# The convolution branch's projection in three passes, a fourth buffer for high weight parts, and VectorE work moved between stages, in a two-block layer stack

## The reference, cut to what matters

```python
mod = silu(c) @ w_ada + b_ada
h = rmsnorm(x, norm_g) * (1 + scale) + shift
rq, rk, rv, rg, xbc, dt_raw, z, fq, fk, fv, fg, f_raw = split(h @ w_in)
xbc = silu(causal_dwconv(xbc, conv_w, conv_b))          # 4 taps
mixed = concat([retention * silu(rg), rmsnorm(ssd * silu(z)), fox * silu(fg)])
x = x + gate * (mixed @ w_out)
```

```python
# GLU -> depthwise conv (31 taps) -> channel layernorm -> swish -> projection
conv = silu(layernorm(dwconv(a * sigmoid(g)))) @ w_conv_out       # 512 -> 1024
mlstm = (rmsnorm(h_fwd + h_bwd) * sigmoid(o_pre)) @ w_mlstm_out   # 4 heads of 256
attn = attention(q, k, v) @ w_attn_out                            # 8 heads, 2 for k and v
x = x + g1 * ((g_conv * conv + g_mlstm * mlstm + g_attn * attn) @ w_out)
x = x + g2 * conv_ffn(h)                                          # 1024 -> 2 x 2816 -> 1024
```

## Time and profile before

| | before |
|---|---|
| median of 3 runs | 2354.2 us (2354.12 to 2355.55) |
| the profiled execution | 2356.64 us, span 2354.8 us |
| granted TensorE clock, mean | 0.987 |
| PE busy | 2293.4 us (97%), 14962 matmuls |
| PEld, DVE, ACT, POOL busy | 81%, 60%, 41%, 5% |

### The profile page before, as it was taken

The page is one execution under the profiler, slowest core; times in us unless marked ns, Lnnn a source line. Parts: engine busy times, 40 slices in busy tenths (PEclk is TensorE's granted clock), DMA queues, the critical chain, the costliest instruction groups (busy, mean ns, idle before and its releaser), DMA issues.

```text
span 2354.8 us, 35094 instructions
## 1 busy us (share of the span) xinstructions
PE 2293.4 (97%) x14962; PEld 1908.9 (81%) x14962; DVE 1411.5 (60%) x2590; ACT 973.0 (41%) x1571; POOL 119.2 (5%) x95
## 2 busy tenths in 40 slices
PE   6999999999999999999999999999999999999999
PEld 4898888988877887776787677775877988998999
DVE  1467844667748676545344555555267757566984
ACT  2438633376524354352221332331244535544542
POOL 0000000000000032120000000000000133100000
PEclk8999999999999999999999999999999999999999
DMA  9794357863444111113332454332333311564553
GB/s 312 248 294 148 104 182 249 288 215 118 134 141 129 49 60 38 48 41 107 107 100 95 144 180 161 125 99 71 99 109 77 97 61 55 165 209 146 190 177 117
DMA packets 335532, 323.25 MB, mean 137 GB/s; under 512 B 28560, under 2 KB 334992, under 8 KB 335248
## 3 DMA queue, kind: packets, MB, share of 16 engines
q1 hardware_dynamic: 335376, 321.00, 43.2%
HBM read 319.93 MB, written 1.05 MB: 136 GB/s over the span
## 4 chain that ended last, share of the span: by engine, by line
PE 89%; DVE 6%; DMA 2%; ACT 2%; issue 0%; POOL 0%; SPq 0%; ACTq 0%
PE ps L746 88%; DVE parts L2031 1%; DMA ring<-w_ada 1%; ACT w_high L1508 1%; DMA ring<-w_in 1%; DVE arena L2416 1%; DVE arena L2572 1%; PE ps L1259 1%; POOL parts L1956 0%; DVE arena L2174 0%; DVE arena L2168 0%; SPq L677 0%; ACT arena L1618 0%; DVE parts L2071 0%; DVE arena L2542 0%
## 5 line engine op out<-in xcount | busy, mean ns | idle before, releaser
L746 PE MATMUL ps<-parts,w_high 128*128 128x256 f32 (+1 forms) x6384 | 1135.3, 327 | 5.2 <-DVE arena L2612 2.3
L746 PEld LDWEIGHTS ps<-parts,w_high 128*128 128x128 f32 x6384 | 950.3, 189 | 137.0 <-issue 27.7
L746 PE MATMUL ps<-parts,parts 128*128 128x256 f32 (+1 forms) x3384 | 609.6, 321 | 6.9 <-DVE parts L2387 2.6
L1508 ACT ACTIVATE w_high<-ring 128x1024 fp32r<-128x1024 f32 (+2 forms) x426 | 433.0, 1026 | 411.0 <-PE ps L746 327.5
L746 PEld LDWEIGHTS ps<-parts,parts 128*128 128x128 f32 x3384 | 502.6, 189 | 63.1 <-DVE parts L2031 3.1
L2387 DVE TENSOR_TENSOR parts<-ring,w_high 128x1024 fp32r<-128x1024 f32 (+2 forms) x262 | 304.6, 1169 | 231.4 <-ACT w_high L1508 230.9
L1956 POOL TENSOR_TENSOR parts<-ring,w_high 128x512 fp32r<-128x512 f32 x88 | 118.3, 1372 | 1899.5 <-ACT w_high L1508 1899.5
L746 PE MATMUL ps<-arena 128*64 128x256 f32 (+7 forms) x928 | 184.0, 397 | 6.5 <-DVE arena L2612 5.9
L746 PEld LDWEIGHTS ps<-arena 128*128 128x128 f32 (+2 forms) x928 | 123.5, 171 | 53.1 <-issue 19.8
L2031 DVE TENSOR_TENSOR parts<-ring,w_high 128x1024 fp32r<-128x1024 f32 x88 | 104.8, 1221 | 96.6 <-ACT w_high L1508 96.6
L2416 DVE SCALAR_TENSOR_TENSOR arena<-arena,cols 128x512 f32<-128x512 f32 (+1 forms) x240 | 158.2, 659 | 6.0
(11 more groups left out here) (270 smaller groups left out, 1794.6 us busy)
## 6 DMA issues: line engine op xcount, KB each, us to landing
ring<-w_in SPq DMA_DIRECT2D x118, 1024.0 KB, 5.3
ring<-ada_w SPq DMA_DIRECT2D x48, 1024.0 KB, 5.5
ring<-ffn_w_up SPq DMA_DIRECT2D x44, 1024.0 KB, 5.1
ring<-w_ada SPq DMA_DIRECT2D x24, 1024.0 KB, 7.5
ring<-w_out SPq DMA_DIRECT2D x16, 1024.0 KB, 5.1
ring<-ffn_w_down SPq DMA_DIRECT2D x16, 1024.0 KB, 5.2
ring<-w_out SPq DMA_DIRECT2D x16, 512.0 KB, 4.4
ring<-w_mlstm_out SPq DMA_DIRECT2D x8, 1024.0 KB, 5.2
```

The source lines that it names most:

```text
L746: return tensor.matmul(o, a, b, start=first, stop=last)
L1508: scalar.activation(half_high(m), half_raw(m), ACT.Copy).then_inc(*a.step(("w_high", m)))
```

## The change

It has these parts.

- Constants: `ones` is one column (it is broadcast in the operand), `blk` two columns, `dup0` and `dup1` are gone, and `ada_y` is one buffer rather than two, with a wait of ACT for the batch before. The first load of constants falls from 294 to 167 columns and the second from 1408 to 1026.
- `SPLIT_BUFS` goes from 3 to 4. With the constants this moves `arena` from byte 120,288 to byte 121,344 of each partition, a multiple of 64. Nothing ahead of `w_high` moves, and `cst` stays a multiple of 64.
- The convolution branch's projection (`bo`, b = 0) goes by three passes: DVE makes `ln_high` and `ln_low` ahead of the gate copies and eight low weight halves of four tiles for each layer, ACT eight more high halves. The mLSTM branch's parts are made at n = 8 and 10 rather than 4 and 6.
- Gates: ACT rounds weights `SPLIT_BUFS - 1` halves ahead.
- First stack: ACT's silu of the convolution's tiles 0 to 7 goes between the `fk` evictions; DVE makes the first low half of `rq` ahead of the low activation tiles.
- Taps: none in the mLSTM stage; in layer 0 eight more early ones among the mix stage's last, in layer 1 five rather than four after each attention job.
- Layer 1: the low part of the second half of each head's `mo` strip moves from POOL to DVE, at the head's start.

```diff
@@ -72,7 +72,7 @@
 _at = 0
-for _name, _n in [("ident", P), ("ones", P), ("freq", 1), ("eps", 1), ("eps_eps", 1), ("eps64", 1), ("pick", 32), ("sign", 1), ("cneg", 1), ("blk", P), ("rota", P), ("rotb", P), ("dup0", P), ("dup1", P),
+for _name, _n in [("ident", P), ("ones", 1), ("freq", 1), ("eps", 1), ("eps_eps", 1), ("eps64", 1), ("pick", 32), ("sign", 1), ("cneg", 1), ("blk", 2), ("rota", P), ("rotb", P), 
                   ("low", P), ("up", P), ("axc", SEQ), ("axs", SEQ)]:
...
@@ -312,7 +310,7 @@
-SPLIT_BUFS = 3
+SPLIT_BUFS = 4
 GATES_WHOLE = 3
@@ -333,7 +331,7 @@
         return "gate", name[1]
-    if name[0] == "bo" and name[2]:
+    if name[0] == "bo":
         return "gate", name[1]
@@ -424,7 +422,7 @@
         csel = sb("csel", [P, KT, ADA_SHIFT + 32])
-        ada_y = sb("ada_y", [P, 2, 256])
+        ada_y = sb("ada_y", [P, 256])
         mod1 = sb("mod1", [P, DEPTH, 24])
@@ -457,6 +455,7 @@
         a_parts = under([P, 2, TT])[0:ROWS, :, :]
+        ln_high, ln_low = mh_high[0], merged_high[0]
         laid.append(1)
...
@@ -633,7 +632,7 @@
                 return KT // 2, 2 * P
-            if name[0] == "bo" and name[2] == 1:
+            if name[0] == "bo" and name[2] < 2:
                 return 4, P
...
@@ -1372,30 +1371,25 @@
                     pe.wait_ge(*when(("lnsq", l, t)))
-                    i = mm(u[:, lo:TT], ones, mv_sq[:, t, lo:TT], t == 0, t == DW_T - 1)
+                    i = mm(u[:, lo:TT], ones.to_broadcast([P, P]), mv_sq[:, t, lo:TT], t == 0, t == DW_T - 1)
                 i.then_inc(*pe.step(("full", ("lnq", l))))
+                ln_tiles = [ln_high[:, k, :] for k in range(4)]
                 att_tiles = [att_high[:, k, :] for k in range(4)]
                 mh_tiles = [mh_high[k // 4][:, k % 4, :] for k in range(KT)]
-                for b, (high, low, parts) in enumerate(((None, None, None), (att_tiles, att_low, ("att", l)), (mh_tiles, mh_low, ("mh", l)))):
+                for b, (high, low, parts) in enumerate(((ln_tiles, ln_low, ("ln", l)), (att_tiles, att_low, ("att", l)), (mh_tiles, mh_low, ("mh", l)))):
                     for s in range(4):
...
                         name = ("bo", l, b, s)
-                        wt = take(name)
+                        take(name)
                         for j in range(2):
                             u = unit(("bo", l, b, 2 * s + j))
-                            if b:
-                                i = split_strip(u[:, lo:TT], name, j, lo, low, high=high, parts=parts)
-                                i.then_inc(*pe.step(("used_half", half_no[name, j]), ("full", ("bo", l, b, 2 * s + j)), ("used", name)))
-                                continue
-                            for k in range(4):
-                                pe.wait_ge(*when(("ln", l, k)))
-                                i = mm(u[:, lo:TT], wt[:, k, j * P:(j + 1) * P], cacc[:, k, lo:TT], k == 0, k == 3)
-                            i.then_inc(*pe.step(("full", ("bo", l, b, 2 * s + j)), ("used", name)))
+                            i = split_strip(u[:, lo:TT], name, j, lo, low, high=high, parts=parts)
+                            i.then_inc(*pe.step(("used_half", half_no[name, j]), ("full", ("bo", l, b, 2 * s + j)), ("used", name)))
                 for s in range(4):
@@ -1468,7 +1462,9 @@
                 a.wait_ge(*when(full(("ada_y", batch))))
-                scalar.activation(ada_y[:, batch % 2, :], bank(("ada_y", batch))[:, 0:256], ACT.Copy).then_inc(*a.step(("ada_y", batch), read(("ada_y", batch))))
+                if batch:
+                    a.wait_ge(*when(full(("ada_m", batch - 1))))
+                scalar.activation(ada_y[:, :], bank(("ada_y", batch))[:, 0:256], ACT.Copy).then_inc(*a.step(("ada_y", batch), read(("ada_y", batch))))
@@ -1588,14 +1584,20 @@
+                def convolved(t0, t1):
+
+                    for t in range(t0, t1):
+                        a.wait_ge(*when(("conv", l, t)))
+                        scalar.activation(xconv[:, t, :], xconv[:, t, :], ACT.Silu, bias=col(g1, "conv_b")[:, t:t + 1]).then_inc(*a.step(("xconv", l, t)))
+
+                convolved(0, 4)
                 for s in range(2):
...
                     scalar.activation(fkT[:, 2 * s:2 * s + 2, :], bank(("fk", l, s)).rearrange("p (a b) -> p a b", a=2), ACT.Copy).then_inc(*a.step(("fk", l, s), read(("fk", l, s))))
-                for t in range(CONV_T):
-                    a.wait_ge(*when(("conv", l, t)))
-                    scalar.activation(xconv[:, t, :], xconv[:, t, :], ACT.Silu, bias=col(g1, "conv_b")[:, t:t + 1]).then_inc(*a.step(("xconv", l, t)))
+                    convolved(4 + 2 * s, 6 + 2 * s)
+                convolved(8, CONV_T)
                 for b in range(2):
@@ -1888,7 +1890,7 @@
                     gate = (0, 2, 1)[b]
-                    high_parts(("gate", l), half_no[("bg", l, b, n // 2 % 4), n % 2] + 2)
+                    high_parts(("gate", l), half_no[("bg", l, b, n // 2 % 4), n % 2] + SPLIT_BUFS - 1)
                     a.wait_ge(*when(full(("bg", l, b, t))))
@@ -1900,6 +1902,7 @@
                     scalar.activation(cacc[:, t, lo:TT], cacc[:, t, lo:TT], ACT.Silu, scale=col(g2, "conv_ln_w_2")[:, t:t + 1], bias=col(g2, "conv_ln_b_2")[:, t:t + 1]).then_inc(*a.step(("ln", l, t)))
+                high_parts(("gate", l), half_no[("bo", l, 0, 1), 0])
                 for t in range(4, 3 * KT):
@@ -1950,6 +1953,8 @@
                 for n in range(first, last_half["back", l] + 1):
+                    if l and split_halves[n][0][0] == "mo" and split_halves[n][1]:
+                        continue
                     p.wait_ge(*when(("w_high", n)))
@@ -2065,12 +2070,14 @@
+                weights_low("rq", 0, (0,))
                 v.wait_ge(*when(full(("fv", l, 1))))
...
-                for part, s in (("rq", 0), ("rq", 1), ("rk", 0), ("rk", 1), ("xbc", 0), ("xbc", 1)):
+                weights_low("rq", 0, (1,))
+                for part, s in (("rq", 1), ("rk", 0), ("rk", 1), ("xbc", 0), ("xbc", 1)):
                     weights_low(part, s)
@@ -2499,6 +2506,7 @@
                     low_part(mix_half + n)
+                    early_taps(0 if lo else 4)
                 axc, axs = const("axc"), const("axs")
@@ -2551,7 +2559,7 @@
                     att_prob(n)
-                    taps(4 if lo else 2)
+                    taps(5 if lo else 2)
                     if n > 2 and n % 2:
@@ -2615,6 +2623,8 @@
                         m_exponents(0, 1)
+                    if l:
+                        low_part(half_no[("mo", l, hd), 1])
                     m_weights(hd, 0)
@@ -2622,7 +2632,6 @@
                         m_exponents(hd + 1, 0)
-                    taps(DW_T * DW_K - taps_done[0] if hd == M_HEADS - 1 else 3)
                     m_outs(hd, 1)
@@ -2661,6 +2670,13 @@
+                for t in range(DW_T):
+                    v.wait_ge(*when(("ln", l, t)))
+                    vector.tensor_copy(ln_high[:, t, lo:TT], cacc[:, t, lo:TT]).then_inc(*v.step(("h_high", "ln", l, t)))
+                    v.wait_ge(*when(("h_high", "ln", l, t)))
+                    vector.tensor_tensor(ln_low[:, t, lo:TT], cacc[:, t, lo:TT], ln_high[:, t, lo:TT].bitcast(F32), ALU.subtract).then_inc(*v.step(("h_low", "ln", l, t)))
+                for j in range(2):
+                    low_part(half_no[("bo", l, 0, 0), j])
                 for t in range(KT):
@@ -2673,8 +2689,8 @@
                             branch_parts("att", aq, 0, att_high, att_low)
-                        if n in (4, 6):
-                            branch_parts("mh", mq, 4 * (n // 6), mh_high[n // 6], mh_low)
+                        if n in (8, 10):
+                            branch_parts("mh", mq, 4 * (n // 10), mh_high[n // 10], mh_low)
                         v.wait_ge(*when(full(("bo", l, b, t))))
@@ -2695,7 +2711,7 @@
                             vector.tensor_tensor(merged_low[:, t, lo:TT], o, high.bitcast(F32), ALU.subtract).then_inc(*v.step(("h_low", "wo2", l, t)))
-                        if 3 <= n // 2 < 11:
+                        if n // 2 < 11:
                             low_part(half_no[("bo", l, (n // 2 + 1) // 4, (n // 2 + 1) % 4), n % 2])
```

More of the change, by code:

```diff
@@ L94, in shape_constants @@
     put("ones", 1.0)
-    put("blk", (p[:, None] // 64 == p[None, :] // 64))
+    put("blk", (p[:, None] // 64 == np.arange(2)[None, :]))
     for name, half in (("rota", 64), ("rotb", 32)):
@@ L492, in program @@
         eps = const("eps")
-        one_col = ones[:, 0:1]
+        one_col = ones
         pick = const("pick")
@@ L801, in ada_sum @@
                 for t in range(2):
-                    i = mm(u[:, 24 * t:24 * t + 24], ada_y[:, batch % 2, t * P:(t + 1) * P], pick[:, 0:24])
+                    i = mm(u[:, 24 * t:24 * t + 24], ada_y[:, t * P:(t + 1) * P], pick[:, 0:24])
                 i.then_inc(*pe.step(("full", ("ada_m", batch))))
@@ L820, in group_sum @@
                 for g in range(4):
```

(5 more changed lines are left out.)

3 lines of the change are left out of this document (removed).

## The result

The changed kernel takes 2339.9 us (median of 4, 2338.7 to 2342.1) against 2354.4: a ratio of 0.9937, with a 95% interval of 0.9926 to 0.9949, so 12 to 17 us less. The prediction was 2324 with a range of 2317 to 2343; its rival (a) said 2340. The profiled execution spans 2338.6 us, 16.2 less than before.

What follows compares the result with a forecast made beforehand. The prediction took TensorE, busy 97% of the span, as the bound. Steps 1 to 6 sum to -14.2 us and step 7 adds -16: -30.2 from the profiled 2356.6 gives 2326.4, a median of 2324, range 2317 to 2343.

Steps and rivals of the forecast that it cites:

- rival (a): The start of `arena` doesn't matter, so the gain of step 7 is missing: 2340 us; chance 0.28.
- step 7: `arena` put on a multiple of 64 bytes: 512-column fp32r matmuls reading it fall to 0.227 us; -16 us, bounds -20 and 0.
- step 6: First stack, silus between the `fk` evictions: VectorE's convolution ends its last tile as late as before; -0.5 us, bounds -2 and 0.
- Steps 1 and 2: Convolution branch's projection of b = 0, fp32 replaced by fp32r passes: -5.4 us in layer 0, -0.5 in layer 1.
- Step 3: Taps out of layer 0's mLSTM stage: TensorE's waits for the outputs shrink; -5.5 us, bounds -6.0 and -4.
- Step 4: Layer 1's mLSTM stage: waits of 2.3 us go, low parts on VectorE cost +2.4; taken as 0, bounds -2 and +2.5.
- Step 5: First low weights of `rq`: their subtraction moves into VectorE's idle time, 1.15 us gained per layer; -2.3 us, bounds 0 and -2.5.
- Rival (c): A TensorE that waits less gets less clock; 2% less mean clock gives 2370 us; chance 0.04.

## Why the prediction was right and wrong

The sign was right; the size was twice too large: -30.2 us forecast, -14.8 measured. The step that failed is step 7 (-16 forecast, -5.9 measured for the shift alone), and step 6 added to it (-0.5 forecast, +5 in the traces). These two make up the miss. The time lay inside the range only because the range had been stretched to reach rival (a). Its ends do not follow from the terms: with every term at its best the sum is 2314 and not 2317, and without the shift and every term at its worst it is 2349 and not 2343.

**Step 7, the operands' place: wrong rule, so wrong size.** The prediction put `arena` on a multiple of 64 bytes and gave every stage the fast pace, -16 us. The shift alone gave -5.9. The trace of before held two facts and I joined them wrongly: that 0.2267 and 0.2327 follow the operand was right, and holds in all twelve kernels; that 32 against 33 pieces of 64 bytes explains it was a number that happened to fit, and only roughly: with two thirds of the operands off it would make 2.1%, and the rows say 2.6%. The runs put another rule in its place: 512-column fp32r matmuls take 0.227 us when the activation tile and the weights start at the same place modulo 256 bytes, 0.229 to 0.234 when they don't. By that rule the change brought only up's tiles into agreement (128 and 128) and left gates and down at 0 against 128, mix at 192 against 128. The part about 256 columns stands: there agreement costs, 0.120 against 0.118 to 0.119. The true size of the idea was near what was claimed, -13.3 to -14.4 us in the kernel before with the tiles really in agreement, so the phenomenon was sized well and its condition was not. The counter-rule that was weighed, lines of 16 bytes in the Trainium skill's page "SBUF — State Buffer", section "Specifications (TRN2)", is no better: read as the prediction read it, no shift of 32 or 128 bytes should matter, and each did. Why agreement matters (for instance whether loads of weights and reads of tiles meet) no run here shows.

**Steps 1 and 2, three passes for b = 0: right.** -5.4 and -0.5 forecast. The two traces before and after drift apart by 5.3 us over layer 0's three groups and by 0.5 over layer 1's. In layer 1 VectorE was late as foreseen, 0.68 us at the first low weights against 0.9. The cover in layer 0 held, and it is as thin as was said. VectorE's first two low weight halves and TensorE's first matmul with low weights, after:

```profile
1063.57 1.29 DVE L2394 TENSOR_TENSOR parts<-ring,w_high 128x512 fp32r<-128x512 f32 x2
...
1064.44 1.10 PE L745 MATMUL ps<-parts 128*128 128x512 f32 x4
```

The first half ends at about 1064.2, 0.2 us before it is read; a tenth was forecast. The undo run gives +2.4 us by its time, with an interval that holds both nothing and the 5.9.

**Step 3, taps in layer 0: right.** -5.5 forecast; the traces move apart by 2.2, 2.2 and 1.4, 5.8 in all, and together again by as much in the undo. Another 1.5 us between the second and the third place are not counted: there the trace of before has a granted clock of 0.72 (978 to 984 us), and the kernel with the shift alone, which runs the same instructions, has 1.00, so it is this execution's chance.

**Step 4, layer 1's mLSTM: near in the sum, but both parts too small.** The taps' waits were 2.3 us by the row, and taking them back costs 3.7 in the trace. The low part on VectorE was put at +2.4 and measures +3.8 at its places in the trace, +5.6 by the ratio: 1.1 of the subtraction's 4.9 us were covered, where half had been put down as covered. Forecast 0, with -2 to +2.5 as bounds; the traces before and after show +0.9 over this stage. That the sum came out is luck, since two misses of 1.4 us cancelled.

**Step 5: right.** -2.3 forecast; the traces step by -1.2 at each of the two places.

**Step 6: wrong sign.** -0.5 forecast; putting the silus back gains 7.5 us by the ratio and 5.0 in the traces. The prediction saw that VectorE's convolution ends no sooner and concluded that nothing is lost. It missed that TensorE's wait, though no later at its end, becomes one long idle stretch instead of many short ones, after which the granted clock is at its lower level for some microseconds. The two traces end 9.0 us apart. They place 2.4 and 2.6 at the silus of the two layers; 2.6 more lie in the first 50 us, where the three kernels above that undo another part and keep the new order are 1.8 to 2.1 us ahead of the changed kernel's trace as well, and the rest in stretches with a clock below 1.00. So what is over 5.0 is not the silus' as far as the traces show.

**Rival (c)** did not come: the mean clock was 0.985 after and 0.987 before. Where it did fall, at the silus, it fell behind a longer single wait. **Rival (a)** named the right time, 2340, and that was luck. The place does matter, and its gain of about 6 us was cancelled by step 6's loss.

**What the parts make together.** Undone one at a time, the effects by the ratios are: shift -5.9 (in the kernel before), b = 0 -2.4, taps -10.6, mo lows +5.6, silus +7.5, and step 5's -2.3 from the trace: -8.1, where the whole is -14.8. Four of these are differences known to some 5 us each, and an error in the changed kernel's ratio enters the sum four times, so the gap of 7 is within the noise. The places in the traces fit better: shift -5.9 (by the ratio), b = 0 -5.8, taps of layer 0 -5.8, layer 1's mLSTM stage +0.9, step 5 -2.3, silus +5.0, together -13.9. The constants' smaller loads and the batch's single `ada_y` were not tried alone.

## What to carry to other kernels

When two stages that run the same instruction show two paces, note where their operands start before looking for a cause, and test by moving one of them by a few bytes: a padding of one line told more here than any argument. A wait that is only gathered, not shortened, can still cost time, so compare the longest idle stretch of TensorE before and after a reordering, and not only the sum. An instruction moved to the head of a stage, where its engine is what the others wait for, should be priced nearly in full (here 3.8 of 4.9 us) and not by half. And when several undo runs share one base, compare traces place by place before adding up ratios.

## What the runs showed that I had not expected

- Agreement modulo 256 bytes between an activation tile and weights in `w_high` and the ring: 24 matmuls of 512 columns in 5.44 us with it, 5.56 to 5.60 without; with 256 columns it costs, 0.120 against 0.118.
- Behind 3.76 us in which TensorE was idle, 32 small matmuls took 2.98 us instead of 1.93, and the window's granted clock was 0.83 instead of 1.00; over all fourteen traces 0.74 to 0.83 against 0.91 to 1.00.
- Ten executions of one program ranged over 10 us (2343 to 2353) in the kernel before with the shift alone; those of the kernel before ranged over 3 us on the same chip, and over 6 and 7 on the two others.
